# Routing the last tile from its scaled rows, with root and shift applied to the logits, and the first expert's gate weights split at other places

## What the reference computes

```
h = rmsnorm(x, g_norm_mix) * (1.0 + sc1) + sh1
x = x + gt1 * hybrid_mixer(h, positions, w_in, w_o)       # ends in the output projection w_o
h = rmsnorm(x, g_norm_ffn) * (1.0 + sc2) + sh2
x = x + gt2 * hier_moe(h, w_router_group, w_router_expert, w_up, w_gate, w_down)
out = rmsnorm(x, g_norm_final)

def rmsnorm(x, g): return x * rsqrt(mean(x * x, axis=-1) + EPS) * g
def hier_moe(tok, ...):     # 4 groups of 8 experts
    grp  = argmax(softmax(tok @ w_router_group))           # 4 logits a row
    fine = (tok @ w_router_expert)[grp]                    # 8 of 32 logits a row
    top_p, top_i = top_k(softmax(fine), 2)
    # each row goes through two experts: (silu(x @ w_gate[e]) * (x @ w_up[e])) @ w_down[e], 512 wide
```

## Time and profile before

| what | value |
|---|---|
| median of 3 runs | 1575.89 us (1575.22 to 1576.64) |
| profiled execution | 1575.17 us, of which span 1573.0 |
| PE busy | 1420.4 us, 90% |
| DVE busy | 1098.9 us, 70% |
| ACT busy | 906.5 us, 58% |
| POOL busy | 272.8 us, 17% |
| DMA | 360.14 MB, mean 229 GB/s |

### The profile page before, as it was taken

How to read it: one execution, slowest core, us unless ns; L and a number is a source line. 1 busy time by engine, 2 the same in 40 slices (tenths; PEclk the granted TensorE clock), 3 DMA queues, 4 the chain that set the end, 5 groups by cost and what they waited for, 6 DMA issues and landing times.

```text
span 1573.0 us, 21452 instructions
## 1 busy us (share of the span) xinstructions
PE 1420.4 (90%) x7388; PEld 1109.4 (71%) x7388; DVE 1098.9 (70%) x1478; ACT 906.5 (58%) x1220; POOL 272.8 (17%) x192
## 2 busy tenths in 40 slices
PE   4899999999999897888899959999999999999980
PEld 2785447888888786556666747888888888888860
DVE  2726996642367984443344378999999999999968
ACT  5513767869974112434444425777777777777732
POOL 0000101320001012100000002232223322233115
PEclk9999999999999898789999979999999999999985
DMA  9213544555524234221111147999999999999986
GB/s 360 92 54 107 163 159 154 208 215 185 196 82 148 63 132 160 92 93 68 54 55 48 51 186 280 384 401 394 409 400 397 396 400 393 398 398 394 397 329 262
DMA packets 99076, 360.14 MB, mean 229 GB/s; under 512 B 11448, under 2 KB 23992, under 8 KB 74304
## 3 DMA queue, kind: packets, MB, share of 16 engines
q1 hardware_dynamic: 74816, 292.13, 49.0%
q0 software_dynamic: 11264, 33.57, 6.2%
q10 hardware_dynamic: 12928, 33.56, 5.4%
HBM read 306.76 MB, written 60.83 MB: 234 GB/s over the span
## 4 chain that ended last, share of the span: by engine, by line
PE 47%; DVE 5%; ACT 3%; issue 2%; DMA 1%; POOL 1%; ACTq 0%; DVEq 0%; POOLq 0%
PE PS L1748 13%; PE PS L1750 13%; PE PS L1749 13%; PE PS L2079 2%; PE PS L1898 1%; PE PS L1987 1%; PE PS L1974 1%; DMA WK<-xn_dram,gidx 1%; PE PS L2123 1%; DVE wlo L1510 1%; PE PS L2068 1%; ACT WK L954 1%; POOL BIG L777 1%; ACT WK L990 1%; DVE WK L1577 1%
## 5 line engine op out<-in xcount | busy, mean ns | idle before, releaser
L1510 DVE TENSOR_TENSOR wlo<-raw,whi 128x2048 fp32r<-128x2048 f32 x190 | 431.4, 2286 | 33.2 <-ACT whi L970 31.2
L970 ACT ACTIVATE whi<-raw 128x2048 fp32r<-128x2048 f32 x190 | 360.5, 1913 | 122.9 <-DVE WK L1673 80.8
L1748 PE MATMUL PS<-whi,xhi 128*128 128x512 f32 x512 | 203.7, 398 | 2.8 <-DVE xlo L1590 2.8
L1750 PE MATMUL PS<-whi,xlo 128*128 128x512 f32 x512 | 200.9, 392 | 0.0
L1749 PE MATMUL PS<-wlo,xhi 128*128 128x512 f32 x512 | 200.1, 391 | 0.0
L904 ACT ACTIVATE KV<-ACC,WK 128x1024 int8<-128x1024 f32 (+4 forms) x160 | 147.5, 925 | 24.7 <-DVE WK L1268 22.0
L744 POOL COPY wcol<-tw 128x1 f32 (+1 forms) x32 | 64.3, 2009 | 358.5 <-DVE WK L1696 358.5
L1748 PE MATMUL PS<-KVR,BIGR 128*128 128x512 f32 x304 | 120.4, 396 | 2.0 <-ACT WK L893 2.0
L1750 PE MATMUL PS<-KVR,BIGR 128*128 128x512 f32 x304 | 118.6, 390 | 0.0
L1749 PE MATMUL PS<-KVR,BIGR 128*128 128x512 f32 x304 | 118.3, 389 | 0.0
L1748 PEld LDWEIGHTS PS<-whi,xhi 128*128 128x128 f32 x512 | 96.9, 189 | 22.7 <-DVE xlo L1590 3.6
(11 more groups left out here) (336 smaller groups left out, 2802.9 us busy)
## 6 DMA issues: line engine op xcount, KB each, us to landing
raw<-in_w_up SPq DMA_DIRECT2D x64, 1024.0 KB, 7.8
raw<-in_w_down SPq DMA_DIRECT2D x64, 1024.0 KB, 7.9
raw<-in_w_gate SPq DMA_DIRECT2D x62, 1024.0 KB, 8.1
WK<-in_w_ada POOLq DMA_DIRECT2D x16, 1024.0 KB, 5.9
y_dram<-zero ACTq DMA_DIRECT2D x8, 2048.0 KB
y_dram<-WK ACTq DMA_DIRECT2D x32, 512.0 KB
KV<-in_w_in SPq DMA_DIRECT2D x5, 2048.0 KB, 9.2
KV<-in_x SPq DMA_DIRECT2D x16, 512.0 KB, 5.2
```

The source lines that it names most:

```text
L970: nc.scalar.activation(whi[:, slot], first_gate[q] if known(i, 1) and q in GATE else raw[:, q], ACT.Copy).then_inc(G("m_hi"), 1)
L1510: V.tensor_tensor(wlo[:, slot], first_gate[q] if known(i, 1) and q in GATE else raw[:, q], whi[:, slot].bitcast(F32), ALU.subtract)\
L1748: mm(out_, x_hi, w_hi, start=first, stop=False)
L1750: return mm(out_, x_lo, w_hi, start=False, stop=final)
```

## The change

Last tile: the product of its residual rows with sc2 (which holds g*(1+sc2) by then) is made by VectorE in each half of `mix`, and `turn` and `route` work on it. The root of the row and the shift's logits, `shift_logits`, are applied by the one operation that copies the logits out of PSUM. The shift's logits are made once, on TensorE, behind the router of tile 6, from `shift_cols`, a copy of the shift that is loaded by columns. The normed rows, still needed for the gather, are made by one operation into a place of their own. The square is taken in two halves. The second half of the last projection gets bank 2. `rank` goes behind `turn`. The first item's GATE halves are cast by ScalarE in the step `rows` of the last tile, the first low part stands ahead of the last `mix`, and the second behind the first item's rows; the high parts use other slots than the low ones, which holds for all items.

```diff
+        shift_cols, shift_logits = [wsc[:, :, :].rearrange("p t h -> p (t h)")[:, a:b] for a, b in ((0, KD), (KD, KD + 36))]
+        last_normed = BIG[:, 22528:23552]
+        squares = BIG[:, 23552:24576]
...
-        between[T] = [[("route", T - 2), ("choose", 0), ("mix", (T - 1, 0))], [("choose", 1), ("mix", (T - 1, 1)), ("rank", 0)],
-                      [("norm", T - 1), ("turn", T - 1)], [("route", T - 1)]]
+        between[T] = [[("route", T - 2), ("choose", 0), ("mix", (T - 1, 0))], [("choose", 1), ("mix", (T - 1, 1))],
+                      [("norm", T - 1), ("turn", T - 1), ("rank", 0)], [("route", T - 1)]]
...
+        def mix_bank(i, h):
+
+            return 2 if (i, h) == (T - 1, 1) else 7
...
+        def high_slot(slot):
+
+            return (slot + 2) % 4
...
@@ sync
                     sp.dma_start(WC["wr"], w_router).then_inc(G("ld_c"), 16)
+                    n = [row for row, _ in LATE].index("sh2")
+                    sp.dma_start(shift_cols, late_dram[n].rearrange("(k p) -> p k", p=P), allow_slow_non_contiguous=True)                        .then_inc(G("ld_c"), 16)
...
-            sp.wait_ge(G("c_x1"), T)
+            sp.wait_ge(G("c_x1"), T + 1)
...
-            sp.wait_ge(G("c_xn"), T + 1)
-            sp.dma_start(xn_dram[tile(TILES[T - 1]), :], WC["sq"]).then_inc(G("st_xn"), 16)
+            sp.wait_ge(G("c_xn"), T + 2)
+            sp.dma_start(xn_dram[tile(TILES[T - 1]), :], last_normed).then_inc(G("st_xn"), 16)
...
@@ scalar, step rows
+                    if i == T - 1:
+                        for q in GATE:
+                            high(0, 0, q)
@@ scalar, step norm
-                    own.go(A(WC["sq"], WC["x"], ACT.Square, accum_out=small[:, 52:53]), G("norm_sq"))
-                    if i == T - 1:
-                        for q in GATE:
-                            high(0, 0, q)
+                    if i < T - 1:
+                        own.go(A(WC["sq"], WC["x"], ACT.Square, accum_out=small[:, 52:53]), G("norm_sq"))
+                    else:
+                        own.go(A(squares[:, 0:512], WC["x"][:, 0:512], ACT.Square, accum_out=small[:, 52:53]))
+                        act.wait_ge(G("c_x1"), T + 1)
+                        own(A(squares[:, 512:D], WC["x"][:, 512:D], ACT.Square, accum_out=small[:, 53:54]), G("norm_sq"))
...
@@ vector, step choose
+                    if i == 0:
+                        low(0, 0, GATE[0])
@@ vector, step mix
+                    if i == T - 1:
+                        own(V.tensor_tensor(WC["sq"][:, part], WC["x"][:, part], WC["sc2"][:, part], ALU.mult), G("c_xn"))
@@ vector, step norm
+                    if i == T - 1:
+                        own(V.tensor_tensor(small[:, 52:53], small[:, 52:53], small[:, 53:54], ALU.add))
...
-                    for a, b in ((0, D),) if i < T - 1 else ((0, 512), (512, D)):
-                        own(V.scalar_tensor_tensor(WC["sq"][:, a:b], WC["x"][:, a:b], small[:, 49:50], WC["sc2"][:, a:b],
-                                                   ALU.mult, ALU.mult))
-                        own(V.tensor_tensor(WC["sq"][:, a:b], WC["sq"][:, a:b], WC["sh2"][:, a:b], ALU.add), G("c_xn"))
-                    if i == T - 1:
-                        for q in GATE:
-                            low(0, 0, q)
+                    if i < T - 1:
+                        own(V.scalar_tensor_tensor(WC["sq"], WC["x"], small[:, 49:50], WC["sc2"], ALU.mult, ALU.mult))
+                        own(V.tensor_tensor(WC["sq"], WC["sq"], WC["sh2"], ALU.add), G("c_xn"))
+                    else:
+                        own(V.scalar_tensor_tensor(last_normed, WC["sq"], small[:, 49:50], WC["sh2"], ALU.mult, ALU.add),
+                            G("c_xn"))
@@ vector, step route
-                    own(V.tensor_copy(L[:, TILES[i], :], PS[:, 7, 0:36]), G("b7_free"))
+                    if i == T - 2:
+                        own(V.tensor_copy(shift_logits, PS[:, 7, 36:72]))
+                    if i < T - 1:
+                        own(V.tensor_copy(L[:, TILES[i], :], PS[:, 7, 0:36]), G("b7_free"))
+                    else:
+                        own(V.scalar_tensor_tensor(L[:, TILES[i], :], PS[:, 7, 0:36], small[:, 49:50], shift_logits,
+                                                   ALU.mult, ALU.add), G("b7_free"))
...
             own(V.tensor_scalar(tbl[:, 0:1], PS[:, 7, 0:1], float(NO_TOKEN), None, ALU.add), G("r_done"))
+            low(0, 0, GATE[1])
...
+                if e == 0:
+                    low_rows(0, 0)
                 own.go(V.tensor_tensor(ohp[:, some], c("iota").unsqueeze(1).to_broadcast([P, 8, P]),
...
-                if e == 0:
-                    low_rows(0, 0)
@@ tensor, step route
+                    if i == T - 2:
+                        for k in range(KD):
+                            last = mm(PS[:, 7, 36:72], shift_cols[:, k:k + 1].to_broadcast([P, P]),
+                                      WC["wr"][:, 36 * k:36 * k + 36], start=(k == 0), stop=(k == KD - 1))
```

More of the change, by code:

```diff
@@ L719, in _ @@
                 own.go(tt(wo_lo[:, k], wo[:, k], wo_hi[k].bitcast(F32), ALU.subtract), G("wo_lo"))
-            pool.wait_ge(G("ld_c"), 16 * 4)
+            pool.wait_ge(G("ld_c"), 16 * 5)
             own(tt(WC["sc2"], WC["sc2"], WC["g"], ALU.mult), G("pool_set"))
@@ L969, in high @@
                     act.wait_ge(G("m_used"), n - 3)
-                nc.scalar.activation(whi[:, slot], first_gate[q] if known(i, 1) and q in GATE else raw[:, q],
+                nc.scalar.activation(whi[:, high_slot(slot)], first_gate[q] if known(i, 1) and q in GATE else raw[:, q],
                                      ACT.Copy).then_inc(G("m_hi"), 1)
@@ L1074, in _ @@
                 high(0, 0, q)
-            act.wait_ge(G("m_lo"), 2)
+            act.wait_ge(G("m_lo"), 1)
             high_rows(0, 0)
@@ L1510, in low @@
                 V.tensor_tensor(wlo[:, slot], first_gate[q] if known(i, 1) and q in GATE else raw[:, q],
-                                whi[:, slot].bitcast(F32), ALU.subtract)\
+                                whi[:, high_slot(slot)].bitcast(F32), ALU.subtract)\
                     .then_inc(G("m_lo"), 1)
@@ L1563, in _ @@
                     dve.wait_ge(G("b7_ready"), at7[("mix", i, h)] + 1)
-                    own(V.tensor_tensor(WC["sq"][:, part], PS[:, 7, :], WC["gt1"][:, part], ALU.mult),
+                    own(V.tensor_tensor(WC["sq"][:, part], PS[:, mix_bank(i, h), :], WC["gt1"][:, part], ALU.mult),
                         G("b7_free"))
                     own(V.tensor_tensor(WC["x"][:, part], WC["x"][:, part], WC["sq"][:, part], ALU.add),
-                        G("c_x1") if h else None)
+                        G("c_x1") if h or i == T - 1 else None)
+                    if i == T - 1:
+                        own(V.tensor_tensor(WC["sq"][:, part], WC["x"][:, part], WC["sc2"][:, part], ALU.mult), G("c_xn"))
                 if kind == "norm":
@@ L2038, in _ @@
                         pe.wait_ge(G("c_yT"), i + 1)
-                    bank7(("mix", i, h))
+                    if mix_bank(i, h) == 7:
+                        bank7(("mix", i, h))
                     part = slice(512 * h, 512 * h + 512)
@@ L2046, in _ @@
                                 pe.wait_ge(G("wo_lo"), k - 3)
-                        last = split_product(PS[:, 7, :], yhi[:, k, :], ylo[:, k, :], wo_hi[k][:, part], wo_lo[:, k, part],
+                        last = split_product(PS[:, mix_bank(i, h), :], yhi[:, k, :], ylo[:, k, :], wo_hi[k][:, part], wo_lo[:, k, part],
                                              k == 0, k == KD - 1)
@@ L2063, in _ @@
                     bank7(("route", i, 0))
-                    pe.wait_ge(G("ld_c"), 16 * 4)
+                    pe.wait_ge(G("ld_c"), 16 * 5)
                     for k in range(KD):
@@ L2115, in rows_half @@
                     last = split_product(PS[:, bank, :], xhi[:, s, 4 * h + k], xlo[:, s, 4 * h + k],
-                                         whi[:, slot, part], wlo[:, slot, part], h == 0 and k == 0, h == 1 and k == 3)
+                                         whi[:, high_slot(slot), part], wlo[:, slot, part], h == 0 and k == 0,
+                                         h == 1 and k == 3)
                 last.then_inc(G("m_used"), 1)
@@ L2137, in down @@
                             kk = 2 * (q % 2) + k
-                            last = split_product(PS[:, 5 + h, :], hhi[:, kk], hlo[:, kk], whi[:, slot, part],
+                            last = split_product(PS[:, 5 + h, :], hhi[:, kk], hlo[:, kk], whi[:, high_slot(slot), part],
                                                  wlo[:, slot, part], kk == 0, kk == KF - 1)
```

2 lines of the change are left out of this document (1 added, 1 removed).

## The result

The changed kernel takes 1580.7 us (median of ten runs, 1576.6 to 1584.8) against 1575.6 for the kernel before (1574.2 to 1577.3): ratio 1.0032, 95% interval 1.002 to 1.0043. The median lies outside the range of 1573.0 to 1578.4 and above the 0.2% up to which I called it "the same". A later session, with twelve runs of it, gave 1578.9 against 1575.9: 1.0019, interval 1.0009 to 1.0029. So the loss is real, and it is 3 to 5 us where I had forecast none.

A forecast was written before the change was run, and what follows sets the result against it. One chain of waits from the last output projection to the first expert was taken as decisive, the TensorE-bound expert loop being untouched. Terms summed to -0.17 to +0.2, taken as 0: 1575.9 us, range 1573.0 to 1578.4.

The forecast's parts named there:

- the same: Outcome class for the whole kernel: a difference within about 0.2% or 3.15 us; chance 0.81.
- The second gate half, 2.3, is put ahead of the block counts ... fills it exactly: list and gather arrive together.: Before the first expert: VectorE's low part uses up the item list's 2.24 slack; list and first gather both at 942.7.
- I take 1.95, since shape and clock are those of 902.23 ... TensorE is 1.2 later, not 2.15.: Behind tile 6's router: extra shift products cost 1.95; TensorE ends the last projection 1.2 late, as its halves no longer wait.
- the late one: VectorE from tile 6's choice to the last projection's second half: no idle, add done at 921.4, x1 2.75 late.
- (a): Rival at last tile's transposes, rank and router: clock stays up or falls late, 2.8 less, 1573.1; chance 0.13, whole or half.
- The second half of the projection follows without a wait: Last projection on TensorE: with bank 2 the 0.88 idle goes; second half takes 5.6, ending at 918.15.
- the store of the normed rows is covered: Ahead of the first table: the store lands by about 931.3, leaving 3 us of cover.
- The transfer of the shift: Load by columns, 1024 single elements: between nothing and 10.6 us, hidden behind GpSimd's 28.47 us of idle.
- (b): Rival at the shift products: the repeated column loads in half the time, 1 us won, 1574.9; chance 0.12.
- (d): Rival before the last projection: VectorE is not late, casts and low part fall into idle time; -2.2, chance 0.03.
- faster: Outcome class for the whole kernel: gain beyond about 3.15 us, from (a) together with (b) or (d); chance 0.11.
- (c): Rival at the second gather: it meets the up weights; +0.3 computed, up to +6.7 (1582.6); chance 0.12 for over 1 us.

The follow-up runs named there:

- both moves: Changed kernel with the second gate half's low part behind the item list and the shift products in TensorE's idle time; ratio 0.9989 to the kernel before.

## Why the prediction was wrong

**The step that failed: "The second gate half, 2.3, is put ahead of the block counts ... fills it exactly: list and gather arrive together."** I counted the low part only against what stands behind it on VectorE. That part was right: the list came at 942.64 plus 0.2, which is 943.4 in the frame of before, where I had said 942.7, and the logits were late by the same 0.7. But the low part also holds GpSimd, which I had not put on the list of those who wait. The gather, said to land at 942.7, landed at 944.8 (945.4 in the frame of before), 2.0 after the list and not with it, and TensorE waited for it. The index copy costs 2.05, the same in either profile, and moving the low part alone takes it back whole. The Trainium skill, "SBUF — State Buffer", section "SBUF: two separate sides", says that VectorE and GpSimd share one pair of ports as an exclusive lock, and that a VectorE operation with two inputs in SBUF and a GpSimd instruction that reads SBUF exclude each other for the whole of whichever starts first. The traces agree: the low part reads `ACC` and `whi`, the copy that starts behind it ends with it (2.23), the issue that starts behind it ends 1.0 after it (2.62 and 2.40), and the copy that starts 0.13 ahead of it takes its usual 0.18. A hint stood in the rows of before. In the expert loop, where VectorE runs such low parts nearly without a break, the copy of the same line, there with a column that is chosen at run time, took 2252 ns in the mean against 0.18 us at its first call, and the first of these ends within 0.04 us of the low parts beside it (the group's line, then one row each of the timelines of VectorE and GpSimd):

```profile
L734 POOL COPY gidx<-tbl 128x1 int32 x28 | 63.0, 2252 | 0.0
...
985.84 4.49 DVE L1510 TENSOR_TENSOR wlo<-raw,whi 128x2048 fp32r<-128x2048 f32 x2
...
988.12 2.25 POOL L734 COPY gidx<-tbl 128x1 int32 x1
```

**The second step that failed: "I take 1.95, since shape and clock are those of 902.23 ... TensorE is 1.2 later, not 2.15."** The products took 1.95, from 1.78 behind the start of the group before them, the first matmul of the projection came at 906.56 in the frame of before (said: 906.7). But I took the clock behind them as given. It fell to half as the projection began, and from the first matmul to VectorE's multiply on the half it took 7.45 instead of 5.99. VectorE, said to be the late one without idle, waited 1.09 for TensorE (913.43) and was 0.95 behind the forecast at that multiply. In the kernel before with the products added, the same stretch took 7.45 as well. In all six profiles with two groups of products in a row the fall stands 7.2 to 7.6 behind the reciprocal; in the four without them there is none at that place. Rival (a) had let the moment differ between executions; between these six it differed by 0.4.

**Right by the rows.** The second half of the projection follows without a wait. By its own rows it takes 5.71 (911.28 to 916.99), not the 5.6 of the prediction, which changes nothing. The choice ended at 910.6 in the frame of before (910.75), its second part took 4.75, the scaled rows of the second half were done at 923.1 (922.15 and the late 0.95). The transposes came at 923.2, the router at 925.3, the logits at 928.9: each within 0.9 of the forecast, the difference being that 0.95. That the store of the normed rows is covered holds: the chain reaches the first table from TensorE's ranks.

```profile
933.15 0.64 PE PS L2024 x2
...
934.73 1.24 DVE WK L1632
937.36 2.24 POOL gidx L747
...
940.46 4.34 DMA WK<-xn_dram,gidx
```

**The transfer of the shift.** GpSimd waits for it, and later has 23.05 us of idle where it had 28.47:

```profile
643.22 2.80 POOL L734 TENSOR_TENSOR BIG<-BIG 128x1024 f32<-128x1024 f32 x1 [6.84 <-DMA wsc<-late_dram]
669.07 0.55 POOL L738 TENSOR_TENSOR small<-small,expo 128x1 f32<-128x1 f32 x1 [23.05 <-DVE small L1597]
```

Most of the difference was there already: GpSimd's operation ahead of this wait began at 626.55 against 623.41 before. The wait itself is 6.84 us against 6.05 before, so the transfer, 8.9 us from issue to landing, is worth 0.8 there, inside the bounds of nothing and 10.6 us, and all of it is hidden.

**The rivals.** (a) A clock that stays up at the router was not seen after, where the second half's transposes were partly warm (0.87 against 1.09) and the router full 3.47. It did occur in one profile, with both moves, worth 1.2. Its chances do not add up as written: (a) at 0.13 together with (b) or (d) is far under the 0.11 given to "faster". (c) The second gather took 3.84 against 3.55, as the +0.3 of the text, and the next 11.02 against 10.59. But in the second profile they took 3.52 and 10.50, so (c) is not shown. There is no gap before the second item's transposes. The gap before the third's was there before, 1.13, and is 1.55 and 1.04 in the two profiles of after:

```profile
972.55 1.16 PE L2079 MATMUL PS<-cst,WK 128*128 128x128 f32 x8 [1.13 <-DMA WK<-xn_dram,gidx]
```

Behind it TensorE is busy without a gap in the loop, as before, and an item takes no longer: the low parts of the third and fourth items' rows are 17.53 apart, against 17.81 before:

```profile
985.00:1500.00 515.00, 515.00 (x2431) 431.12 (x2430) 489.03 (x290) 384.99 (x261) 150.66 (x85) 1.00 1.00 397
```

The sum of after, from its own two profiles, is then +0.5 at the logits, +2.05 at the copy, 0.4 to 0.9 up to the third item, and 0.2 to 0.3 back: +3.3 and +2.8 at the last item.

**What stays open.** In the session of the result the medians differ by 5.1, in the next by 3.0, and the profiles account for about 3 only; the rest of the 5.1 has no cause shown. Single runs of the same kernel follow the clock that was granted over all of it (the correlation of time with mean clock is -0.71 over 35 runs of before), and falls in earlier stages come and go; why is not settled, and so neither are the 2 us between the sessions, which need not have run on the same chip. Nor is it settled why the third item of the kernel with both moves lost 2.5. And no run tells whether it is the width of the 36-column products or only their number that brings the clock down.

## What to carry to other kernels

When a long VectorE operation with two operands in SBUF is moved, look at what GpSimd does in that stretch, not only at VectorE's own queue: a 0.2 us copy or the issue of an indirect transfer beside it can cost nearly the whole 2.3 us (2.05 for the copy here), and if a gather hangs on it, the chain pays. A small operation's mean in a busy stretch against the same operation in a quiet one (2252 ns against 180) points at such a lock before any edit, though here the two were not quite the same form. Work that is cheap by its duration can cost more by what it does to the clock behind it; a place where TensorE idles anyway is better for narrow products than one where it would go straight on to wide ones, here 2.0 us of work and 1.1 to 1.4 more of clock.

## What the runs showed of the hardware

Besides the lock: the granted clock of TensorE fell behind 3.73 us of back-to-back 36-column products, in which its records leave no gap, and not behind 1.95 us of them. It fell within 0.3 us of the first 512-column matmul behind them, stayed at half for 3.4 us, and rose again, in six profiles of six, at distances from the reciprocal that differ by 0.4 at most. And moving a blocked GpSimd copy to VectorE did not free GpSimd: the issue of the indirect transfer went from 1.15 to 2.62 us, as the next thing to be held by the same VectorE operation.
